# A down projection as seven block products, with the weight sums made by adding transfers

## What is computed

```python
    h = rms_norm(x, ffn_norm[l])
    g = jnp.einsum('bsd,df->bsf', h, w_gate[l])          # 1024 -> 2816
    u = jnp.einsum('bsd,df->bsf', h, w_up[l])
    x = x + jnp.einsum('bsf,fd->bsd', jax.nn.silu(g) * u, w_down[l])   # 2816 -> 1024
```

## Time and profile before

| | |
|---|---|
| median of 3 runs | 641.24 us (640.96 to 641.27) |
| span of the profiled execution | 638.8 us |
| PE busy | 619.9 us, 97% of the span |
| DVE busy | 438.6 us, 69% |
| ACT busy | 285.1 us, 45% |
| down projection, first to last matmul | from 512.18 to 635.23 us of the span |

### The profile page before, as it was taken

The page is one execution under the profiler, slowest core; times in us unless marked ns, Lnnn a source line. Parts: engine busy times, 40 slices in busy tenths (PEclk is TensorE's granted clock), DMA queues, the critical chain, the costliest instruction groups (busy, mean ns, idle before and its releaser), DMA issues.

```text
span 638.8 us, 10365 instructions
## 1 busy us (share of the span) xinstructions
PE 619.9 (97%) x3840; PEld 528.1 (83%) x3840; DVE 438.6 (69%) x772; ACT 285.1 (45%) x493; POOL 0.2 (0%) x4
## 2 busy tenths in 40 slices
PE   6999999999998989999999999999999999999998
PEld 5866777676867767879999999999999978888886
DVE  4867778685877788777987878788787653233333
ACT  5354536454463645445555444545436432222220
POOL 0000000000000000000000000000000000000000
PEclk9999999999999999999999999999999999999999
DMA  8313032240413241407031233322233432230003
GB/s 309 106 54 111 15 118 62 70 128 4 132 26 107 62 168 40 161 0 264 34 132 69 86 113 133 132 71 97 98 132 132 166 101 97 100 99 1 1 7 125
DMA packets 25591, 61.65 MB, mean 97 GB/s; under 512 B 3024, under 2 KB 3408, under 8 KB 25552
## 3 DMA queue, kind: packets, MB, share of 16 engines
q1 hardware_dynamic: 25552, 61.11, 28.2%
HBM read 54.80 MB, written 2.10 MB: 89 GB/s over the span
## 4 chain that ended last, share of the span: by engine, by line
PE 88%; DVE 7%; ACT 2%; issue 2%; DMA 0%; DVEq 0%; ACTq 0%; SPq 0%
PE ps L1276 26%; PE ps L1278 25%; PE ps L1277 25%; PE ps L1340 3%; PE ps L1353 2%; PE ps L1308 2%; PE ps L1370 1%; DVE w_lo L841 1%; PE ps L1417 1%; ACT probs L534 1%; PE ps L1378 1%; DVE w_lo L823 1%; PE ps L1599 1%; DMA ident<-ident 0%; DVE residual L1092 0%
## 5 line engine op out<-in xcount | busy, mean ns | idle before, releaser
L1276 PE MATMUL ps<-h_sum_parts,w_hi 128*128 128x256 f32 x432 | 120.6, 279 | 0.7 <-ACT q_kept L718 0.7
L1278 PE MATMUL ps<-h_sum_parts,w_lo 128*128 128x256 f32 x432 | 120.9, 280 | 0.0
L1277 PE MATMUL ps<-h_sum_parts,w_hi 128*128 128x256 f32 x432 | 120.5, 279 | 0.0
L841 DVE TENSOR_TENSOR w_lo<-w_raw,w_hi 128x1024 fp32r<-128x1024 f32 x39 | 47.5, 1223 | 53.8 <-ACT w_hi L496 53.8
L1276 PE MATMUL ps<-h_parts,w_hi 128*128 128x512 f32 x192 | 81.5, 424 | 2.4 <-DVE h_parts L958 2.0
L1276 PEld LDWEIGHTS ps<-h_sum_parts,w_hi 128*128 128x128 f32 x432 | 80.8, 187 | 0.9 <-ACT q_kept L718 0.9
L1277 PEld LDWEIGHTS ps<-h_sum_parts,w_hi 128*128 128x128 f32 x432 | 81.2, 188 | 0.0
L1278 PEld LDWEIGHTS ps<-h_sum_parts,w_lo 128*128 128x128 f32 x432 | 81.1, 188 | 0.0
L1278 PE MATMUL ps<-h_parts,w_lo 128*128 128x512 f32 x192 | 75.5, 393 | 0.0
L841 DVE TENSOR_TENSOR w_lo<-w_raw_odd,w_hi 128x1024 fp32r<-128x1024 f32 x37 | 45.2, 1222 | 43.9 <-ACT w_hi L496 43.9
L1277 PE MATMUL ps<-h_parts,w_hi 128*128 128x512 f32 x192 | 75.2, 392 | 0.0
(11 more groups left out here) (157 smaller groups left out, 1099.0 us busy)
## 6 DMA issues: line engine op xcount, KB each, us to landing
w_raw<-wt SPq DMA_DIRECT2D x66, 512.0 KB, 4.0
w_raw_odd<-wt SPq DMA_DIRECT2D x32, 512.0 KB, 3.6
residual<-x SPq DMA_DIRECT2D x4, 512.0 KB, 5.0
q_rotated<-q_gained SPq DMA_DIRECT2D x32, 64.0 KB, 2.0
k_rotated<-k_gained SPq DMA_DIRECT2D x32, 64.0 KB, 2.0
out<-residual SPq DMA_DIRECT2D x8, 256.0 KB, 2.0
ffn_gain<-gain SPq DMA_DIRECT2D x1, 512.0 KB, 3.5
cos<-cos SPq DMA_DIRECT2D x1, 256.0 KB, 6.9
```

The source lines that it names most:

```text
L841: nc.vector.tensor_tensor(WL[:, n % SLOTS], product_source(n), WH[:, n % SLOTS].bitcast(F32), ALU.subtract).then_inc(c_lo, 1)
L1276: nc.tensor.matmul(dst, lh, rh, start=start, stop=False, skip_group_check=True)
L1277: nc.tensor.matmul(dst, lh, rl, start=False, stop=False, skip_group_check=True)
L1278: return nc.tensor.matmul(dst, ll, rh, start=False, stop=stop, skip_group_check=True)
```

## The change

The down projection becomes the same seven-product scheme. The hidden values are cut in four blocks H(row, token), by even and odd hidden tiles (row 0, 1) and by token halves (0, 1); `w_down` is cut in B11, B12 (even tiles; first, second column half) and B21, B22 (odd tiles). The products, in the order in which they are run (`DOWN`):

- P1 = H(0,0) B11; P2 = H(1,0) B21
- P5 = S1 (B11 + B12), with S1 = H(0,1) - H(1,1)
- P6 = S2 (B11 + B12 + B22), with S2 = S1 - H(0,0)
- P3 = S4 B22, with S4 = S2 + H(1,0)
- P7 = S3 (B22 + B12), with S3 = H(0,0) - H(0,1)
- P4 = H(1,1) (B11 + B12 + B22 + B21)

Each product runs over 11 pairs of tiles, in six chunks c: five of two pairs and one of a single pair. A step is one chunk of one product; there are 42 (`STEPS`). A full step has 2 pairs x 2 token tiles x 3 = 12 matmuls of 512 columns, a short one (c = 5) has 6.

The raw slot of chunk c of B11 is kept for the whole stage. When its split for P1 is done, GpSimd issues a transfer that adds B12's chunk onto it; after P5's split one that adds B22's, after P6's split one that adds B21's. B22's slots get B12 added after P3's split. So there are 24 adding transfers, 512 KB for a full chunk and 256 KB for a short one, beside 18 plain loads of the same sizes, where before there were 22 plain loads of 512 KB. Six more raw slots (`LATE`) and the hidden sums (`SN`) lie over the gate stage's `SC`; `AR` moves over `A1`.

The four hidden sums are made by DVE in two parts each (6 and 5 pairs: 1536 and 1280 values per partition), and finished PSUM pairs are added to or taken from `X` by seven `fold`s of 1024 values per partition, both placed between the splits; P6 gathers onto P1's banks, P7 onto both, P3 onto P5's. The last step gathers P4 in banks 6 and 7, which DVE adds to `X` as before, 512 columns each. `TAIL` is 2 steps, nine matmuls per bank as before. The core of the diff (waits of the loads and the sum helpers shortened):

```diff
+DOWN = ("P1", "P2", "P5", "P6", "P3", "P7", "P4")
+CHUNKS = (UNITS + 1) // 2
+STEPS = len(DOWN) * CHUNKS
+SUM_HALF = UNITS // 2 + 1
...
-        AR, _ = place("hidden_parts", [P, SLOTS, 2, SEQ], F32R, r0)
+        LATE = [place(f"down_raw_{n}", [P, D], F32, r0 + (4 * n if n < 5 else 34) * KB)[0] for n in range(6)]
+        SN, _ = place("hidden_sums", [P, UNITS, HALF], F32, r0 + 22 * KB)
...
+        AR, _ = place("hidden_parts", [P, SLOTS, 2, SEQ], F32R, r0 + 106 * KB)
...
+        @block.gpsimd
+        def _(pool):
+            def add_to_sums(q, role, c):
+                pool.wait_ge(c_lo, PRODUCTS + step_at(q, c) + 1)
+                pool.dma_start(down_raw("B11", c).rearrange("p (f n) -> p f n", n=SEQ), down_rows(role, c),
+                               accum_op=ALU.add).then_inc(tb_added[c], 16)
+            for c in range(CHUNKS):
+                add_to_sums("P1", "B12", c)
+            for c in range(CHUNKS):
+                add_to_sums("P5", "B22", c)
+            for c in range(CHUNKS):
+                add_to_sums("P6", "B21", c)
+            for c in range(CHUNKS):
+                pool.wait_ge(c_lo, PRODUCTS + step_at("P3", c) + 1)
+                pool.dma_start(down_raw("B22", c).rearrange("p (f n) -> p f n", n=SEQ), down_rows("B12", c),
+                               accum_op=ALU.add).then_inc(t3_added[c], 16)
...
+            def down_hi(s):
+                n, q, c = PRODUCTS + s, DOWN[s // CHUNKS], s % CHUNKS
+                act.wait_ge(c_used, done(n - SLOTS))
+                if q in ("P1", "P2", "P3"):
+                    down_raw_wait(act, {"P1": "B11", "P2": "B21", "P3": "B22"}[q], c)
+                if q in ("P5", "P6", "P4"):
+                    act.wait_ge(tb_added[c], {"P5": 16, "P6": 32, "P4": 48}[q])
+                if q == "P7":
+                    act.wait_ge(t3_added[c], 16)
+                nc.scalar.activation(WH[:, n % SLOTS, 0:chunk_pairs(c) * SEQ], down_source(q, c),
+                                     ACT.Copy).then_inc(c_hi, 1)
...
-                if n >= PRODUCTS - 2:
-                    hidden_hi(n - (PRODUCTS - 2))
+                if n + SLOTS < PRODUCTS:
+                    product_hi(n + SLOTS)
+                else:
+                    down_hi(n + SLOTS - PRODUCTS)
+                    hidden_hi(n + SLOTS - PRODUCTS)
...
+            for s in range(SLOTS, STEPS):
+                down_lo(s)
+                hidden_lo(s)
+                if s == step_at("P2", 2):
+                    hidden_sum_1(1)
+                if s == step_at("P2", 3):
+                    fold("P1", 0, 0, 0, ALU.add, x11a_s)
+                if s == step_at("P2", 4):
+                    hidden_sum_1(2)
+                if s == step_at("P2", 5):
+                    hidden_sum_3(1)
+                if s == step_at("P5", 1):
+                    hidden_sum_3(2)
+                if s == step_at("P5", 2):
+                    hidden_sum_2(1)
+                if s == step_at("P5", 3):
+                    dve.wait_ge(x11a_s, 1)
+                    fold("P2", 0, 0, 2, ALU.add, y_add)
+                if s == step_at("P5", 5):
+                    hidden_sum_2(2)
+                if s == step_at("P6", 2):
+                    hidden_sum_4(1)
+                if s == step_at("P6", 3):
+                    fold("P5", 1, 1, 4, ALU.add, x22a_s)
+                if s == step_at("P6", 5):
+                    hidden_sum_4(2)
+                if s == step_at("P3", 3):
+                    fold("P6", 0, 1, 0, ALU.subtract, x12a_s)
...
+                if s == step_at("P4", 3):
+                    dve.wait_ge(x22a_s, 1)
+                    fold("P7", 1, 1, 0, ALU.subtract, y_add)
+                    fold("P7", 1, 0, 0, ALU.add, x21a_s)
...
+            def down(s, pair, t):
+                q, c = DOWN[s // CHUNKS], s % CHUNKS
+                n = (PRODUCTS + s) % SLOTS
+                bank = {"P1": 0, "P6": 0, "P7": 0, "P2": 2, "P5": 4, "P3": 4, "P4": 6}[q]
+                qs, cs = slice(pair * HALF + t * P, pair * HALF + (t + 1) * P), slice(pair * SEQ, (pair + 1) * SEQ)
+                begin = q in ("P1", "P2", "P5", "P4") and c == 0 and pair == 0
+                return product(ps[:, bank + t], AR[:, s % SLOTS, 0, qs], AR[:, s % SLOTS, 1, qs],
+                               WH[:, n, cs], WL[:, n, cs], begin, c == CHUNKS - 1 and pair == chunk_pairs(c) - 1)
...
+            TAIL = 2
+            for s in range(STEPS - TAIL):
+                down_ready(s)
...
+                for pair in range(chunk_pairs(s % CHUNKS)):
+                    for t in range(2):
+                        ins = down(s, pair, t)
+                ins.then_inc(c_used, 1)
```

More of the change, by code:

```diff
@@ L106, in done, with step_at, chunk_pairs, tenant @@
     return n + AGAIN + 1
+DOWN = ("P1", "P2", "P5", "P6", "P3", "P7", "P4")
+CHUNKS = (UNITS + 1) // 2
+STEPS = len(DOWN) * CHUNKS
+HOMES = {("B11", c): c for c in range(CHUNKS)} | {("B21", c): 6 + c for c in range(CHUNKS)} | {
+    ("B22", c): (12, 13, 6, 7, 8, 9)[c] for c in range(CHUNKS)}
+SUM_HALF = UNITS // 2 + 1
+def step_at(q, c):
+    return DOWN.index(q) * CHUNKS + c
+def chunk_pairs(c):
+    return min(2, UNITS - 2 * c)
+def tenant(home, role):
+    return 1 + (role == "B22" and home in (6, 7, 8, 9))
 def build(nc, x, wt, vec, gain2, lams, ident_in, mask_in, cos_in, sin_in, out):
@@ L294, in build @@
         ah_s, al_s = sem("hidden_hi_ready"), sem("hidden_lo_ready")
+        late_in = [sem(f"down_raw_in{n}") for n in range(6)]
+        tb_added = [sem(f"down_sum_added{c}") for c in range(CHUNKS)]
+        t3_added = [sem(f"down_raw_added{c}") for c in range(CHUNKS)]
+        s1_s, s2_s_, s3_s, s4_s = (sem(f"hidden_sum_{n}") for n in (1, 2, 3, 4))
+        x11a_s, x12a_s, x22a_s = sem("p1_added"), sem("p16_taken"), sem("p5_added")
+        x21a_s = sem("p167_added")
         y_done = sem("down_rows")
@@ L442, in _ @@
                     sp.dma_start(G2[:], gain2).then_inc(gain2_in, 16)
[L443 to L449, removed]
-            sp.wait_ge(stored, 16 * 2 * TT)
+            for role in ("B11", "B21", "B22"):
+                for c in range(CHUNKS):
+                    down_load(role, c)
+            for n, (tt, half, added) in enumerate(((0, 0, 1), (1, 0, 1), (0, 1, 2), (1, 1, 2), (2, 1, 3), (3, 1, 3),
+                                                   (2, 0, 4), (3, 0, 5))):
+                sp.wait_ge(y_add, added)
+                sp.dma_start(out[tt, :, half * SEQ:(half + 1) * SEQ],
+                             X[:, tt, half * SEQ:(half + 1) * SEQ]).then_inc(stored, 16)
+            sp.wait_ge(stored, 16 * 2 * TT)
+        @block.gpsimd
[10 more added lines that the diff above has]
+                add_to_sums("P6", "B21", c)
+            for c in range(CHUNKS):
+                pool.wait_ge(c_lo, PRODUCTS + step_at("P3", c) + 1)
+                pool.dma_start(down_raw("B22", c).rearrange("p (f n) -> p f n", n=SEQ), down_rows("B12", c),
+                               accum_op=ALU.add).then_inc(t3_added[c], 16)
         @block.scalar
@@ L783, in _ @@
                     silu_first(u + 1)
-                product_hi(n + 4)
-                if n >= PRODUCTS - 2:
-                    hidden_hi(n - (PRODUCTS - 2))
[L787 to L790, removed]
+                if n + SLOTS < PRODUCTS:
[4 more added lines that the diff above has]
+            for s in range(SLOTS, STEPS):
+                down_hi(s)
+                hidden_hi(s)
         @block.vector
@@ L1193, in hidden_whole, with down_lo @@
                                         ALU.mult).then_inc(hid_s, 1)
[L1195 to L1199, removed]
+            def down_lo(s):
+                n, q, c = PRODUCTS + s, DOWN[s // CHUNKS], s % CHUNKS
+                cs = slice(0, chunk_pairs(c) * SEQ)
+                dve.wait_ge(c_hi, n + 1)
+                nc.vector.tensor_tensor(WL[:, n % SLOTS, cs], down_source(q, c), WH[:, n % SLOTS, cs].bitcast(F32),
+                                        ALU.subtract).then_inc(c_lo, 1)
@@ new lines, in hidden_lo, with part_pairs, hidden_sum_1 @@
+            def hidden_lo(s):
+                dve.wait_ge(ah_s, s + 1)
+                nc.vector.tensor_tensor(hidden_part(s, 1), hidden_source(DOWN[s // CHUNKS], s % CHUNKS),
+                                        hidden_part(s, 0).bitcast(F32), ALU.subtract).then_inc(al_s, 1)
+            def part_pairs(part):
+                return (0, SUM_HALF) if part == 1 else (SUM_HALF, UNITS - SUM_HALF)
+            def hidden_sum_1(part):
+                first, count = part_pairs(part)
+                dve.wait_ge(c_used, done(PRODUCTS - 1))
+                dve.wait_ge(hid_s, 2 * (first + count))
+                nc.vector.tensor_tensor(SN[:, first:first + count], hidden_block(0, 1, first, count),
+                                        hidden_block(1, 1, first, count), ALU.subtract).then_inc(s1_s, 1)
@@ new lines, in hidden_sum_3, with hidden_sum_2 @@
+            def hidden_sum_3(part):
```

(67 more changed lines are left out.)

101 lines of the change are left out of this document (69 added, 32 removed).

## The result

The new kernel takes 625.22 us (median of 4 runs, 624.43 to 626.27) against 641.10 us of the kernel before in the same comparison: a ratio of 0.9752, 95% interval 0.9738 to 0.9766. A second comparison on another chip gave 624.28 against 641.07 us, 0.9743 (0.9728 to 0.9757). The forecast was 624.9 us.

The account below looks back on a forecast made before the run. The prediction took PE's matmuls alone to bound the down projection: span 638.8 - 15.4 (matmuls) - 0.9 (first wait) = 622.5 us, with the 2.4 us from span to median 624.9 us; 8 in 10 range 622.5 to 648 us.

Parts of the forecast that it names:

- 66 x 0.2335 = 15.4 us: Down projection on PE: 528 matmuls become 462, each priced at 0.2335 us from start to start, 15.4 us less.
- The first wait: PE's 0.9 us wait at the down projection's start, for the low part of the hidden values, was to go.
- The neighbouring 0.7 us: PE's 0.7 us wait inside the last unit of the gate stage was to neither grow nor go.
- The 2.4 us added to it: The profiled span is 2.4 us under the median time; this distance was kept, taking 622.5 to 624.9 us.
- two passes of the earlier trace: Adding transfers of 512 KB: two passes of 1.54 us, 3.1 us each, overlapping one another.
- at most 6 us after issue: Expected sign on GpSimd's queue: adds land at most 6 us after issue, not later from one to the next.
- the sign that the prediction named for slow adds: Adds' landings move back step by step from P5 to P3 and PE first waits at P7.
- The free budget: Before P7's last full chunk stand 16 adds; 3.4 us an add are free, each us above costs 16 us.
- The load: DVE's work per product: 15.4 us in P2 against PE's 15.4, 15.2 in P5, 13.8 in P6; costed at nothing.
- cushion "of four prepared steps, up to 11 us": Four steps prepared ahead of PE, up to 11 us, were to cover DVE where it is as full as PE.
- Rival (c): DVE becomes the bound in P2 and P5, by 2 us: 626.9 us; chance 0.06.
- Rival (d): DVE shuts GpSimd out, which issues only while DVE rests; 10 us missing in P5, P6, P3: 634.9 us; chance 0.03.

## Why the prediction was right

**Matmuls.** 66 x 0.2335 = 15.4 us was the term that carries the sum; the stage shrank by 15.5, and leaving out 66 matmuls alone gives nearly the same time (0.9758 of the kernel before, against 0.9752). The step that mattered was to take the pitch and not the duration.

**The first wait.** 0.9 us forecast; the wait is gone in both kernels that move the copies. The neighbouring 0.7 us stayed, as said.

**From the span to the time.** The span was forecast at 622.5 us and measured at 622.6, which is the closer test. The 2.4 us added to it set one profile's span against a median of other executions. Every execution's time is 1.7 to 1.9 us above its own span, in all runs here, and the last store lands within the span (issued at 636.38 us and 2.0 us on its way, of 638.8). That the median came within 0.3 us of 624.9 is therefore partly luck: with 1.8 us the sum gives 624.3.

**The adds.** The size was off, on the safe side. An add occupies the engines for 2.55 us in a full queue (0.524 MB at 205 GB/s), where two passes of the earlier trace rows had made 3.1. The term that was too large is the pass: the share of the earlier trace rows makes it 1.54 us, but in a full queue of plain loads a pass takes 1.34 us (512 KB at the 390 GB/s shown below), and two of these are 2.7. The landings were not "at most 6 us after issue" either. P5's first four, with few in flight, land 5.4 to 6.4 us after their issue; P1's adds, beside the plain loads, 7.7 to 14.0; and all from P5's last two on, 9 to 11. Half of the sign that the prediction named for slow adds, landings that move back, thus showed without any wait at P7. With nothing else in flight one lands after 5.4 us:

```profile
w_raw_odd<-wt POOLq DMA_DIRECT2D x1, 512.0 KB, 5.4
```

The free budget was off the other way: 3.4 us an add reckoned, about 3.1 measured. The conclusion held since 2.55 lies below both; at the forecast 3.1 the adds would have stood at the very edge. Which product waits, how many chunks stand before it and what each us costs was borne out by the runs with more adds.

**DVE.** The load was nearly right. P2's 15.4 us busy of 15.4 can't show more than the stretch is long, but P2, P5 and P6 together have 45.1 us, against 15.4 + 15.2 + 13.8 = 44.4. The step that failed is the cushion "of four prepared steps, up to 11 us". A slot is refilled only when PE has left it, and ACT's copy and DVE's two parts come after that. In P3, P7 and P4 operands are therefore ready mostly 3.9 to 4.9 us before PE takes up a full step, and with DVE full, in P5 and at the start of P6, the lead shrinks to as little as 1.6 us. Nothing was lost by it here, but the runs with more work show that 3.4 us more on DVE cost 1.9 us, where by the forecast's cushion they would have cost nothing. Rival (c) was nearer than its 0.06.

**GpSimd.** An issue of 1.2 us was hidden. Rival (d) is ruled out by rows: an add issued while DVE never rests (first row) takes as long as one issued beside a DVE that rests a quarter of the time, and in P5 GpSimd is busy with seven issues while DVE rests for 0.07 us.

```profile
542.10 1.20 POOL L528 DMA_DIRECT2D w_raw_odd<-wt  x1 [0.54 <-DVE w_lo L1312]
...
579.14 1.20 POOL L539 DMA_DIRECT2D down_raw<-wt  x1 [1.66 <-DVE w_lo L1312]
```

This agrees with what the Trainium skill, SBUF — State Buffer, section "Who interferes with whom", says of the two: that `tensor_tensor` does not hold up the making of descriptors. The rule of the Trainium skill, Collectives: The Full Stack, section "The bandwidth ceiling: the fold count and why AG ≠ RS ≠ AR", that the second source halves the rate, is stated there for the reduce-scatter among cores; it nearly fits this transfer too. The adds ran at 205 GB/s, and plain transfers in a full queue at the start of the stage, in the kernel with plain loads, at 390, a factor of 1.9:

```profile
516.00:525.00 9.00, 9.00 (x40) 7.24 (x40) 5.26 (x7) 4.70 (x8) 2.01 (x3) 1.00 1.04 390
```

## What to carry to other kernels

Price an instruction that is pipelined by the distance between starts in a stretch without waits; a count removed from a stage that it bounds comes back in full. An operation moved off the compute engines into transfers is free as long as its rate, not its landing, fits between the step that releases it and the step that needs it: count the transfers that stand before the tightest deadline, and count all others on the same engines too. The deadline sum found the right place here, but its budget was 10% too generous, so leave a margin of that order. And judge a ring's cushion by how long operands lie ready before they are used, not by the number of slots: here four slots gave 1.6 us where DVE was full. A median goes with a median and a span with a span; the step from one to the other is read from one and the same execution.

## What was not expected of the hardware

An adding transfer of 512 KB from HBM takes 2.55 us of all 16 DMA engines in a full queue, 1.9 times a plain one, and 1.2 us of GpSimd for its issue (0.72 for a plain one).

A wait of PE costs more than itself. At the full clock the two starts behind it come about 0.25 us late in all. After a rest of 12.2 us the granted clock stood at 0.50 as well, and the next matmuls started 0.43 us apart until some 5 us had passed.

TensorE's clock was not the same at the start of every profile. PE waits there for the first data, and in the stretch from 10 to 20 us the granted clock is 0.83 in the first profile of the kernel with plain loads, and 1.00 in the new kernel's second profile, of the same program up to that point:

```profile
10.00:20.00 10.00, 6.68 (x24) 5.21 (x23) 8.68 (x16) 7.57 (x11) 0.00 (x0) 0.83 0.57 218
```

```profile
10.00:20.00 10.00, 7.64 (x40) 6.03 (x39) 8.73 (x16) 7.89 (x12) 0.00 (x0) 1.00 0.58 215
```

The down projection starts at 512.56 us in the first and at 511.36 us in the second, and lasts 107.56 us in both. Of the nine profiles of the new kernel and its variants, the four with 0.83 in that stretch start it at 512.6 to 512.9 us, and the five with 1.00 at 511.4 to 511.5. What decides between the two was not tried.
